# High and low split weights word by word in one buffer, and split products that run from the last column to the first

## The chip, the cores and the metric

The kernel runs on one core of one Trainium2 chip. A run's time is the device time of that core in microseconds. Two runs of the kernel before are shown; the trace is of a third, profiled execution.

## The reference

The reference computes three transformer layers, one after the other, on one sequence of 512 tokens with 1024 channels, all in float32. What matters here is that nearly all arithmetic is products of the activations with weight matrices:

```python
h = rms_norm(x, pre_mix_norm)
proj = h @ w_in                              # 1024 -> 6,688 channels
mix = jnp.concatenate([o_a, o_s], axis=-1) @ w_out      # after gated delta net and SSD
x = x + rms_norm(mix, post_mix_norm)
u = causal_dwconv(h @ w_up, ffn_conv_w, ffn_conv_b)     # 1024 -> 2 * 2816
gate, up = jnp.split(u, 2, axis=-1)
f = (jax.nn.silu(gate) * up) @ w_down                   # 2816 -> 1024
return x + rms_norm(f, post_ffn_norm)
```

The second and third layers have the same form with a stick-breaking attention plus pooling, and a gated linear attention, in place of the first mixer, and each has its own feed-forward part.

## The kernel before

**Tiling.** Activations lie with the channels on the 128 partitions and the 512 tokens along the free axis, so a tensor of 1024 channels is 8 tiles of 128x512 (`tile(t, k)`, 2048 bytes a partition each). Weights come in units: 128 output channels, with 8 tiles (KD, 1024 words a partition) or 11 tiles (HALF, 1408 words, for the down projections) of 128x128.

**Split products.** To keep float32 accuracy with TensorE's faster float32r operands, a value is held as two float32r parts, high and low. A product of a weight tile with an activation tile is three matmuls of 512 columns, one behind the other: high weights by high activations, high by low, low by high. All three add into one PSUM bank. In `multiply` they are lines L255, L256 and L257; `fan` (L231 to L233), `begin_pe` (L1466 to L1468) and `mix_pe` (L2634 to L2636) have the same three. Activations in two parts are HH/HL, MH/ML, PH/PL, DH/DL and FH/FL, whose tiles are read with their 512 columns in rising order.

**How a unit is made.** SyncE loads it into one of four `raw` buffers. ScalarE's `split_hi` (L187) copies it into `whi` as float32r. VectorE's `split_lo` (L193) takes `raw - whi` into `wlo`. There are two `whi` and two `wlo` buffers (SPLIT = 2), each one contiguous run of words, so `split_hi` of unit u waits until TensorE has finished unit u-2 (`unit_done`), `split_lo` waits for `split_hi`, and TensorE waits for `split_lo` (`w_lo_ready`). Ten units at the starts of stages go into `first` buffers and two into `early` buffers, likewise in pairs.

**What else the engines do.** In the up projections VectorE scales a finished bank by the norm factor (L390), makes the low part of the unit after next (L193), and does two convolution taps (L464, L468); ScalarE does the high part (L187), the first tap (L438), and for each pair of units a SiLU (L443) and a copy (L447). In the gated delta net (the "GDN" stretch, up to about 350 us) VectorE also inverts small triangular blocks (L1675, L1678, and a transposing copy L1681).

**Plain products.** Products of plain float32 operands leave two records each in the trace, each with a weight load of its own: L2138 with 512 columns, L1728 with 128 columns, among others.

The order on every engine is the order of the program's text; no scheduler moves anything.

Of the kernel before, what the change touches and what calls it, by code (L numbers as in the profile page):

```python
# [64 lines left out]
def program(nc, x_in, w8, w11, par_in, cst_in, small_in, out, plan):  # L65
    cols = columns()
    ctx = ExitStack()
    with ctx:
# [30 lines left out]
        neg_lower, neg_ones, hidden = (cst[:, k * P:(k + 1) * P] for k in range(12, 15))  # L99
        level = [cst[:, (5 + k) * P:(6 + k) * P] for k in range(7)]  # L100
# [25 lines left out]
        for at0 in (0, 8, 16):  # L126
            first_weights[at0] = [tuple(place(f"first_{n}{at0}_{j}", KD * P, FREE + (at0 + 4 * j + 2 * m) * TILE, F32R)
                                        for m, n in enumerate(("hi", "lo"))) for j in range(2)]
# [27 lines left out]
        NORM_COLUMNS, ALL_PARAMS = 9, 16 * 9  # L156
# [24 lines left out]
        def split_hi(act, u, i, per, kt, first=None, behind=SPLIT):  # L181

            hi = whi[u % SPLIT] if first is None else first[0]
            act.wait_ge(raw_in[u % RAW], at(16 * (u // RAW + 1), i, 16 * per // RAW))
            if u >= behind and first is None:
                act.wait_ge(unit_done, at(u - behind + 1, i, per))
            nc.scalar.activation(hi[:, 0:kt * P], raw[u % RAW][:, 0:kt * P], ACT.Copy).then_inc(w_hi_ready, 1)  # L187

        def split_lo(dve, u, i, per, kt, first=None, behind=SPLIT):

            hi, lo = (whi[u % SPLIT], wlo[u % SPLIT]) if first is None else first
            dve.wait_ge(w_hi_ready, at(u + 1, i, per))
            nc.vector.tensor_tensor(lo[:, 0:kt * P], raw[u % RAW][:, 0:kt * P],  # L193
                                    hi[:, 0:kt * P].bitcast(F32), ALU.subtract).then_inc(w_lo_ready, 1)
# [27 lines left out]
        def fan(pe, c, hi, lo, ready, after=None):  # L222

            u0, n = c["u"], c["fan"]
            w = [c["first"][j] if j < 2 else (whi[(u0 + j) % SPLIT], wlo[(u0 + j) % SPLIT]) for j in range(n)]
            pe.wait_ge(w_lo_ready, u0 + n)
            for k in range(KD):
                pe.wait_ge(ready[0], ready[1] + k + 1)
                for j in range(n):
                    a, (wh, wl) = c["spare"][j], (x[:, k * P:(k + 1) * P] for x in w[j])  # L230
                    nc.tensor.matmul(a[:, :], wh, tile(hi, k), start=k == 0, stop=False)  # L231
                    nc.tensor.matmul(a[:, :], wh, tile(lo, k), start=False, stop=False)  # L232
                    last = nc.tensor.matmul(a[:, :], wl, tile(hi, k), start=False, stop=k == KD - 1)  # L233
                    if k == KD - 1:
                        last.then_inc(unit_done, 1)
                if after and k in after:
                    after[k]()

        def multiply(pe, u, t, i, per, per_t, kt, hi, lo, start=True, stop=True, ready=None, part=None, c=None):
# [11 lines left out]
            for k in range(kt) if part is None else range(kt * part // 4, kt * (part + 1) // 4):  # L251
                if ready:
                    pe.wait_ge(ready[0], ready[1] + k + 1)
                wh, wl = whi[w][:, k * P:(k + 1) * P], wlo[w][:, k * P:(k + 1) * P]
                nc.tensor.matmul(a[:, :], wh, tile(hi, k), start=start and k == 0, stop=False)  # L255
                nc.tensor.matmul(a[:, :], wh, tile(lo, k), start=False, stop=False)  # L256
                last = nc.tensor.matmul(a[:, :], wl, tile(hi, k), start=False, stop=stop and k == kt - 1)  # L257
# [11 lines left out]
        def norm_pe(pe, c):  # L269
# [6 lines left out]
        early = [tuple(place(f"early_{n}{j}", KD * P, FREE + (24 + 4 * j + 2 * m) * TILE, F32R)  # L276
                       for m, n in enumerate(("hi", "lo"))) for j in range(2)]
# [886 lines left out]
        def sb_pool(pool, c):  # L1164
# [15 lines left out]
            nc.gpsimd.tensor_copy(sb_cr[:, P:4 * P], cst[:, 12 * P:15 * P]).then_inc(b_const, 1)  # L1180
# [16 lines left out]
        def sb_pe(pe, c):  # L1197
# [114 lines left out]
            busy(bank[0], whi[(u0 + 11) % SPLIT], 12)  # L1312
# [137 lines left out]
        def begin_pe(pe, c):  # L1450

            for k in range(KD):
# [8 lines left out]
                for m in range(2):  # L1462
# [3 lines left out]
                    nc.tensor.matmul(a[:, :], wh, tile(HH, k), start=k == 0, stop=False)  # L1466
                    nc.tensor.matmul(a[:, :], wh, tile(HL, k), start=False, stop=False)
                    last = nc.tensor.matmul(a[:, :], wl, tile(HH, k), start=False, stop=k == KD - 1)  # L1468
# [672 lines left out]
        def load_l1(sp, c):  # L2141
# [39 lines left out]
            for n, k in enumerate(place_of, 1):  # L2181
# [441 lines left out]
        def mix_pe(pe, c):  # L2623
            for m, (k, h) in enumerate(MIX):
# [5 lines left out]
                for j in range(KD):  # L2630
                    if m in (0, 4):
                        pe.wait_ge(h_ready, c["h"] - 2 * KD + h * KD + j + 1)
                    wh, wl = whi[w][:, j * P:(j + 1) * P], wlo[w][:, j * P:(j + 1) * P]
                    nc.tensor.matmul(a[:, :], wh, tile(hi, j), start=h == 0 and j == 0, stop=False)  # L2634
                    nc.tensor.matmul(a[:, :], wh, tile(lo, j), start=False, stop=False)  # L2635
                    last = nc.tensor.matmul(a[:, :], wl, tile(hi, j), start=False, stop=h == 1 and j == KD - 1)  # L2636
# [342 lines left out]
```

## Time and profile before

| | us |
|---|---|
| median of two runs | 2149.45 (2145.89 to 2153.01) |
| the profiled execution, its own time | 2152.09 |
| its span, first to last instruction | 2150.3 |
| TensorE busy | 2102.0 (98%) |
| VectorE busy | 1212.8 (56%) |
| ScalarE busy | 905.8 (42%) |

The profiled execution is 1.8 us longer than its span and lies inside the range of the two runs. TensorE's busy time is a union of overlapping records, so it shows that the engine had work, not how fast that work went: the distance between the starts of neighbouring matmuls tells that. PEclk, or the granted clock, is the share of 2.4 GHz that TensorE was granted; its mean over the span is 0.993.

### The profile page before, as it was taken

The page shows a single profiled execution, that of the slowest core. Times are in us where ns is not written, and L with a number is a line of the kernel's source. Part 1 is how long each engine was busy: PE and PEld are TensorE (multiplying, and loading weights), DVE is VectorE, ACT ScalarE, POOL GpSimd, SP SyncE. Part 2 cuts the span into 40 slices and gives each one's busy share as a digit, 9 for nine tenths or more (in the row PEclk, how much of TensorE's full clock was granted, in tenths as well). Part 3 has the DMA queues.
Part 4 walks back from the last instruction along what each step waited for, and adds up shares of the span by engine and source line. Part 5 has one row for each costly group of instructions (what it writes and reads, how often), then busy time and mean ns, then how long its engine had stood idle before and what let it go on. Part 6 is the DMA issues. An engine that isn't in the chain of part 4 may idle for free.

```text
span 2150.3 us, 26841 instructions
## 1 busy us (share of the span) xinstructions
PE 2102.0 (98%) x9776; PEld 1702.9 (79%) x9776; DVE 1212.8 (56%) x1663; ACT 905.8 (42%) x1282; POOL 325.0 (15%) x266
## 2 busy tenths in 40 slices
PE   6999999999999999999999999999999999999999
PEld 5778888878868888887766888888878878888887
DVE  5898755755366666225544566653354465666522
ACT  6883444434254444224555444442242254444421
POOL 0001121210112222001302122220000012222200
PEclk9999999999999999999999999999999999999999
DMA  7323222122223333222211333232222122333321
GB/s 235 93 77 93 75 75 79 49 69 69 91 66 98 98 98 115 99 80 69 66 43 40 98 98 96 93 119 95 86 69 89 60 70 97 98 97 96 116 95 66
DMA packets 81481, 188.96 MB, mean 88 GB/s; under 512 B 19824, under 2 KB 40432, under 8 KB 81392
## 3 DMA queue, kind: packets, MB, share of 16 engines
q1 hardware_dynamic: 81392, 187.75, 27.7%
q8 instruction: 59, 0.97, 0.2%
q14 instruction: 30, 0.25, 0.0%
HBM read 178.28 MB, written 9.44 MB: 87 GB/s over the span
## 4 chain that ended last, share of the span: by engine, by line
PE 91%; DVE 5%; ACT 2%; issue 1%; DMA 0%; POOL 0%; SPq 0%; DVEq 0%; ACTq 0%
PE acc L255 23%; PE acc L257 23%; PE acc L256 23%; PE bank L1247 1%; PE bank L231 1%; PE bank L233 1%; PE bank L232 1%; PE acc L2636 1%; PE acc L2634 1%; PE acc L2635 1%; PE bank L2019 1%; PE bank L1728 1%; DVE wlo L193 1%; PE bank L255 1%; PE bank L256 1%
## 5 line engine op out<-in xcount | busy, mean ns | idle before, releaser
L255 PE MATMUL acc<-HH,whi 128*128 128x512 f32 x1600 | 643.6, 402 | 6.9 <-DVE wlo L193 4.3
L257 PE MATMUL acc<-HH,wlo 128*128 128x512 f32 x1600 | 625.7, 391 | 0.0
L256 PE MATMUL acc<-HL,whi 128*128 128x512 f32 x1600 | 624.7, 390 | 0.0
L187 ACT ACTIVATE whi<-raw 128x1024 fp32r<-128x1024 f32 (+1 forms) x293 | 324.0, 1107 | 566.1 <-PE acc L257 536.8
L193 DVE TENSOR_TENSOR wlo<-raw,whi 128x1024 fp32r<-128x1024 f32 (+1 forms) x293 | 400.8, 1369 | 283.0 <-ACT whi L187 283.0
L255 PEld LDWEIGHTS acc<-HH,whi 128*128 128x128 f32 x1600 | 301.9, 189 | 73.8 <-DVE wlo L193 10.3
L257 PEld LDWEIGHTS acc<-HH,wlo 128*128 128x128 f32 x1600 | 301.2, 188 | 64.2
L256 PEld LDWEIGHTS acc<-HL,whi 128*128 128x128 f32 x1600 | 302.0, 189 | 62.6 <-issue 4.1
L255 PE MATMUL acc<-FH,whi 128*128 128x512 f32 x528 | 205.8, 390 | 0.0
L256 PE MATMUL acc<-FL,whi 128*128 128x512 f32 x528 | 205.4, 389 | 0.0
L257 PE MATMUL acc<-FH,wlo 128*128 128x512 f32 x528 | 205.4, 389 | 0.0
L390 DVE TENSOR_TENSOR acc<-acc,rs 128x512 f32<-128x512 f32 x150 | 104.8, 698 | 175.7 <-PE acc L257 175.7
L482 POOL TENSOR_TENSOR taps<-taps,taps 128x512 f32<-128x512 f32 x66 | 85.3, 1292 | 507.5 <-DVE taps L468 452.5
L447 ACT ACTIVATE FH<-taps 128x512 f32 (+1 forms) x66 | 41.8, 633 | 199.3 <-POOL taps L482 199.3
L255 PEld LDWEIGHTS acc<-FH,whi 128*128 128x128 f32 x528 | 99.1, 188 | 20.9 <-issue 0.2
L256 PEld LDWEIGHTS acc<-FL,whi 128*128 128x128 f32 x528 | 99.1, 188 | 20.8 <-issue 0.2
L257 PEld LDWEIGHTS acc<-FH,wlo 128*128 128x128 f32 x528 | 99.1, 188 | 20.5
L345 POOL TENSOR_TENSOR hn<-hn,sq 128x512 f32<-128x512 f32 x24 | 36.7, 1528 | 410.9 <-ACT sq L338 410.9
L468 DVE SCALAR_TENSOR_TENSOR taps<-acc,par,taps 128x510 f32<-128x510 f32 x117 | 87.6, 749 | 14.7 <-DVE taps L464 0.5
L487 POOL TENSOR_TENSOR FL<-taps,FH 128x512 f32 (+1 forms) x66 | 85.5, 1295 | 59.9 <-ACT FH L447 59.9
L438 ACT ACTIVATE taps<-acc,par 128x512 f32<-128x512 f32 x117 | 89.0, 761 | 0.6 <-DVE acc L390 0.6
L464 DVE SCALAR_TENSOR_TENSOR taps<-acc,par,taps 128x511 f32<-128x511 f32 x117 | 86.6, 740 | 0.0
(394 smaller groups left out, 2674.4 us busy)
## 6 DMA issues: line engine op xcount, KB each, us to landing
raw<-w SPq DMA_DIRECT2D x257, 512.0 KB, 3.5
raw<-w SPq DMA_DIRECT2D x48, 704.0 KB, 4.0
X<-x SPq DMA_DIRECT2D x4, 512.0 KB, 5.2
x_dram<-small SPq DMA_DIRECT2D x8, 256.0 KB, 4.7
xt_dram<-small SPq DMA_DIRECT2D x8, 256.0 KB, 4.5
a_dram<-l_am SPq DMA_DIRECT2D x8, 256.0 KB, 3.6
l_xt<-xt_dram SPq DMA_DIRECT2D x8, 256.0 KB, 3.3
l_x<-x_dram SPq DMA_DIRECT2D x8, 256.0 KB, 3.1
```

The lines of the kernel that those rows point to most:

```text
L187: nc.scalar.activation(hi[:, 0:kt * P], raw[u % RAW][:, 0:kt * P], ACT.Copy).then_inc(w_hi_ready, 1)
L193: nc.vector.tensor_tensor(lo[:, 0:kt * P], raw[u % RAW][:, 0:kt * P], hi[:, 0:kt * P].bitcast(F32), ALU.subtract).then_inc(w_lo_ready, 1)
L255: nc.tensor.matmul(a[:, :], wh, tile(hi, k), start=start and k == 0, stop=False)
L256: nc.tensor.matmul(a[:, :], wh, tile(lo, k), start=False, stop=False)
L257: last = nc.tensor.matmul(a[:, :], wl, tile(hi, k), start=False, stop=stop and k == kt - 1)
L390: nc.vector.tensor_tensor(a[:, :], a[:, :], rs[:, :], ALU.mult).then_inc(scaled, 1)
L438: nc.scalar.activation(taps[j][:, :], a[:, :], ACT.Identity, scale=w(2), bias=w(3)).then_inc(tap_ready, 1)
L447: nc.scalar.activation(o, taps[j - 1][:, :], ACT.Copy).then_inc(fh_ready, 1)
L464: nc.vector.scalar_tensor_tensor(out=taps[j][:, 1:S], in0=a[:, 0:S - 1], scalar=w(1), in1=taps[j][:, 1:S], op0=ALU.mult, op1=ALU.add).then ...
L468: nc.vector.scalar_tensor_tensor(out=taps[j][:, 2:S], in0=a[:, 0:S - 2], scalar=w(0), in1=taps[j][:, 2:S], op0=ALU.mult, op1=ALU.add).then ...
L482: nc.gpsimd.tensor_tensor(taps[2 * b][:, :], taps[2 * b][:, :], taps[2 * b + 1][:, :], ALU.mult).then_inc(prod_ready, 1)
L487: nc.gpsimd.tensor_tensor(o, taps[2 * b][:, :], h.bitcast(F32), ALU.subtract).then_inc(f_ready, 1)
```

## The change

It has three parts.

1. The pairs `whi[j]`, `wlo[j]` become one buffer `split[j]`: word 0 is the high part of weight 0, word 1 its low part, word 2 the high part of weight 1, and so on. `parts` gives the two views, each with every second word. So ScalarE writes, VectorE reads and writes, and TensorE loads weights with a step of two words. The `first` and `early` buffers are laid out in the same way.
2. `flipped` reverses the 512 columns of both the activation tile and the PSUM bank in every split product, so column 511 goes first. The result is the same.
3. Where a unit begins in `split[j]` depends on the buffer and the unit's length (`SHIFT`, in words: 64 and 32 for units of 8 tiles, 96 and 16 for 11). The room for it comes from constants that are no longer kept: `cst` is 10 tiles in place of 15, loaded by two transfers in place of one. The start of the free region stays a multiple of 512 bytes from that of HH, and is now a multiple of 2048.

```diff
-        whi = [fixed(f"whi{j}", [P, HALF * P], F32R) for j in range(SPLIT)]
-        wlo = [fixed(f"wlo{j}", [P, HALF * P], F32R) for j in range(SPLIT)]
-        cst = fixed("cst", [P, 15 * P])
+        split = [fixed(f"split{j}", [P, 2 * HALF * P + P], F32R) for j in range(SPLIT)]
+        SHIFT = {KD: (64, 32), HALF: (96, 16)}
+
+        def weights(w, kt):
+
+            o = SHIFT[kt][w]
+            return parts(split[w][:, o:o + 2 * kt * P])
+
+        def parts(pair):
+
+            both = pair.rearrange("p (c m) -> p m c", m=2)
+            return both[:, 0, :], both[:, 1, :]
+
+        def flipped(t):
+
+            return t[:, ::-1]
+
+        cst = fixed("cst", [P, 10 * P])
...
-            hi = whi[u % SPLIT] if first is None else first[0]
+            hi = (weights(u % SPLIT, kt) if first is None else first)[0]
...
-            hi, lo = (whi[u % SPLIT], wlo[u % SPLIT]) if first is None else first
+            hi, lo = weights(u % SPLIT, kt) if first is None else first
...
-                wh, wl = whi[w][:, k * P:(k + 1) * P], wlo[w][:, k * P:(k + 1) * P]
-                nc.tensor.matmul(a[:, :], wh, tile(hi, k), start=start and k == 0, stop=False)
-                nc.tensor.matmul(a[:, :], wh, tile(lo, k), start=False, stop=False)
-                last = nc.tensor.matmul(a[:, :], wl, tile(hi, k), start=False, stop=stop and k == kt - 1)
+                wh, wl = (x[:, k * P:(k + 1) * P] for x in weights(w, kt))
+                nc.tensor.matmul(flipped(a), wh, flipped(tile(hi, k)), start=start and k == 0, stop=False)
+                nc.tensor.matmul(flipped(a), wh, flipped(tile(lo, k)), start=False, stop=False)
+                last = nc.tensor.matmul(flipped(a), wl, flipped(tile(hi, k)), start=False, stop=stop and k == kt - 1)
...
-                    sp.dma_start(cst[:, 2 * P:], cst_in[:, 2 * P:]).then_inc(params_in, 16)
+                    sp.dma_start(cst[:, 2 * P:5 * P], cst_in[:, 2 * P:5 * P]).then_inc(params_in, 16)
+                    sp.dma_start(cst[:, 5 * P:], cst_in[:, 10 * P:]).then_inc(params_in, 16)
```

No instruction changes its place on an engine. On TensorE, in a projection of the second layer, these five rows stood before:

```order
3013 L255 MATMUL acc<-HH,whi_58 128x512
3014 L256 MATMUL acc<-HL,whi_58 128x512
3015 L257 MATMUL acc<-HH,wlo_60 128x512
3016 L255 MATMUL acc<-HH,whi_58 128x512
3017 L256 MATMUL acc<-HL,whi_58 128x512
```

and now, with the high and the low part under one name:

```order
3013 L270 MATMUL acc<-HH,split_58 128x512
3014 L271 MATMUL acc<-HL,split_58 128x512
3015 L272 MATMUL acc<-HH,split_58 128x512
3016 L270 MATMUL acc<-HH,split_58 128x512
3017 L271 MATMUL acc<-HL,split_58 128x512
```

The same instructions stand in the same order; only operands differ. The one instruction more in the whole program is on SyncE, the second transfer of constants near the start.

## Rows read from the trace of the kernel before

**Rows 1.** The page: busy time, granted clock by slice, chain by engine.

```profile
PE 2102.0 (98%) x9776; PEld 1702.9 (79%) x9776; DVE 1212.8 (56%) x1663; ACT 905.8 (42%) x1282; POOL 325.0 (15%) x266
...
PEclk9999999999999999999999999999999999999999
...
PE 91%; DVE 5%; ACT 2%; issue 1%; DMA 0%; POOL 0%; SPq 0%; DVEq 0%; ACTq 0%
```

**Rows 2.** Timeline, first up projection: start us, us, engine, line, operation.

```profile
699.63 0.39 PE L255 MATMUL acc<-HH,whi 128*128 128x512 f32 x1
...
700.08 0.39 PE L257 MATMUL acc<-HH,wlo 128*128 128x512 f32 x1
700.08 0.19 PEld L255 LDWEIGHTS acc<-HH,whi 128*128 128x128 f32 x1
700.31 0.39 PE L255 MATMUL acc<-HH,whi 128*128 128x512 f32 x1
...
705.75 0.39 PE L255 MATMUL acc<-HH,whi 128*128 128x512 f32 x1
```

**Rows 3.** Groups by line and form: the high (L187) and low (L193) parts.

```profile
L193 DVE TENSOR_TENSOR wlo<-raw,whi 128x1024 fp32r<-128x1024 f32 x245 | 322.8, 1319 | 154.8 <-ACT whi L187 154.8
L187 ACT ACTIVATE whi<-raw 128x1024 fp32r<-128x1024 f32 x245 | 257.8, 1054 | 371.7 <-PE acc L257 342.5 <-PE acc L2636 11.9 <-PE bank L233 8.6
L193 DVE TENSOR_TENSOR wlo<-raw,whi 128x1408 fp32r<-128x1408 f32 x48 | 78.0, 1625 | 128.2 <-ACT whi L187 128.2
L187 ACT ACTIVATE whi<-raw 128x1408 fp32r<-128x1408 f32 x48 | 66.2, 1379 | 194.4 <-PE acc L257 194.4
...
L193 DVE TENSOR_TENSOR first_lo<-raw,first_hi 128x1024 fp32r<-128x1024 f32 x10 | 11.8, 1222 | 13.1 <-ACT first_hi L187 13.1
...
L193 DVE TENSOR_TENSOR early_lo<-raw,early_hi 128x1024 fp32r<-128x1024 f32 x2 | 2.4, 1222 | 0.3 <-ACT early_hi L187 0.3
```

**Rows 4.** The chain in order of time, plain float32 products: start us, us, what.

```profile
193.44 0.89 PE bank L1728 x8
...
201.13 0.86 PE bank L2138 x2
```

**Rows 5.** Timeline of VectorE over two units of the up projection.

```profile
701.87 0.70 DVE L390 TENSOR_TENSOR acc<-acc,rs 128x512 f32<-128x512 f32 x1 [0.65 <-PE acc L257]
703.04 1.22 DVE L193 TENSOR_TENSOR wlo<-raw,whi 128x1024 fp32r<-128x1024 f32 x1 [0.48 <-ACT whi L187]
...
705.07 0.75 DVE L468 SCALAR_TENSOR_TENSOR taps<-acc,par,taps 128x510 f32<-128x510 f32 x1
707.31 0.70 DVE L390 TENSOR_TENSOR acc<-acc,rs 128x512 f32<-128x512 f32 x1 [1.49 <-PE acc L257]
708.97 1.55 DVE L193 TENSOR_TENSOR wlo<-raw,whi 128x1024 fp32r<-128x1024 f32 x1 [0.96 <-ACT whi L187]
...
712.75 0.70 DVE L390 TENSOR_TENSOR acc<-acc,rs 128x512 f32<-128x512 f32 x1 [0.67 <-PE acc L257]
```

**Rows 6.** Windows of the GDN and the second up projection: busy us of each engine.

```profile
core 0: us, PE busy (x) PEld busy (x) DVE busy (x) ACT busy (x) POOL busy (x), PEclk, DMA share, GB/s
100.00:172.00 72.00, 68.31 (x342) 54.50 (x341) 69.00 (x139) 52.03 (x81) 3.60 (x4) 1.00 0.32 90
1195.00:1436.00 241.00, 241.00 (x1061) 198.85 (x1060) 151.38 (x175) 100.48 (x133) 54.41 (x42) 1.00 0.31 98
```

**Rows 7.** The same GDN window, instructions of line L193 alone.

```profile
100.00:172.00 72.00, 10.30 (x9) 1.00 0.32 90
```

**Rows 8.** Line L1681: duration ns min/median/max, first and last start, forms.

```profile
L1681 DVE COPY l_blk<-small x3: 1062/1108/1118, 156.4 to 284.5; 48x1024 f32<-48x1024 f32 x2, 32x1024 f32<-32x1024 f32 x1
```

More of the change, by code:

```diff
@@ L97, in program @@
         ident, ones, upper, lower, halves = (cst[:, k * P:(k + 1) * P] for k in range(5))
-        neg_lower, neg_ones, hidden = (cst[:, k * P:(k + 1) * P] for k in range(12, 15))
-        level = [cst[:, (5 + k) * P:(6 + k) * P] for k in range(7)]
+        neg_lower, neg_ones, hidden = (cst[:, k * P:(k + 1) * P] for k in range(7, 10))
+        level = {5 + k: cst[:, (5 + k) * P:(6 + k) * P] for k in range(2)}
         def col(name, k=0, n=1):
@@ L126, in program @@
         for at0 in (0, 8, 16):
-            first_weights[at0] = [tuple(place(f"first_{n}{at0}_{j}", KD * P, FREE + (at0 + 4 * j + 2 * m) * TILE, F32R)
-                                        for m, n in enumerate(("hi", "lo"))) for j in range(2)]
+            first_weights[at0] = [parts(place(f"first_{at0}_{j}", 2 * KD * P, FREE + (at0 + 4 * j) * TILE, F32R)[:, :])
+                                  for j in range(2)]
         acc = [ctx.enter_context(nc.psum_tensor(f"acc{j}", [P, S], F32)) for j in range(2)]
@@ L224, in fan @@
             u0, n = c["u"], c["fan"]
-            w = [c["first"][j] if j < 2 else (whi[(u0 + j) % SPLIT], wlo[(u0 + j) % SPLIT]) for j in range(n)]
+            w = [c["first"][j] if j < 2 else weights((u0 + j) % SPLIT, KD) for j in range(n)]
             pe.wait_ge(w_lo_ready, u0 + n)
@@ L230, in fan @@
                     a, (wh, wl) = c["spare"][j], (x[:, k * P:(k + 1) * P] for x in w[j])
[L231 to L233 removed]
+                    nc.tensor.matmul(flipped(a), wh, flipped(tile(hi, k)), start=k == 0, stop=False)
+                    nc.tensor.matmul(flipped(a), wh, flipped(tile(lo, k)), start=False, stop=False)
+                    last = nc.tensor.matmul(flipped(a), wl, flipped(tile(hi, k)), start=False, stop=k == KD - 1)
                     if k == KD - 1:
@@ L275, in program @@
         NARROW = 32
-        early = [tuple(place(f"early_{n}{j}", KD * P, FREE + (24 + 4 * j + 2 * m) * TILE, F32R)
-                       for m, n in enumerate(("hi", "lo"))) for j in range(2)]
+        early = [parts(place(f"early_{j}", 2 * KD * P, FREE + (24 + 4 * j) * TILE, F32R)[:, :]) for j in range(2)]
         tab_w = place("tab_w", KD * NARROW, FREE + 17 * TILE)
@@ L1311, in sb_pe @@
             pe.wait_ge(w_lo_ready, u0 + 12)
-            busy(bank[0], whi[(u0 + 11) % SPLIT], 12)
+            busy(bank[0], weights((u0 + 11) % SPLIT, KD)[0], 12)
             for i in range(NP):
@@ L1465, in begin_pe @@
                         pe.wait_ge(w_lo_ready, m + 1)
-                    nc.tensor.matmul(a[:, :], wh, tile(HH, k), start=k == 0, stop=False)
-                    nc.tensor.matmul(a[:, :], wh, tile(HL, k), start=False, stop=False)
-                    last = nc.tensor.matmul(a[:, :], wl, tile(HH, k), start=False, stop=k == KD - 1)
+                    nc.tensor.matmul(flipped(a), wh, flipped(tile(HH, k)), start=k == 0, stop=False)
+                    nc.tensor.matmul(flipped(a), wh, flipped(tile(HL, k)), start=False, stop=False)
+                    last = nc.tensor.matmul(flipped(a), wl, flipped(tile(HH, k)), start=False, stop=k == KD - 1)
                     if k == KD - 1:
@@ L2632, in mix_pe @@
                         pe.wait_ge(h_ready, c["h"] - 2 * KD + h * KD + j + 1)
[L2633 to L2636, printed above, removed]
+                    wh, wl = (x[:, j * P:(j + 1) * P] for x in weights(w, KD))
+                    nc.tensor.matmul(flipped(a), wh, flipped(tile(hi, j)), start=h == 0 and j == 0, stop=False)
+                    nc.tensor.matmul(flipped(a), wh, flipped(tile(lo, j)), start=False, stop=False)
+                    last = nc.tensor.matmul(flipped(a), wl, flipped(tile(hi, j)), start=False, stop=h == 1 and j == KD - 1)
                 last.then_inc(unit_done, 1)
```

6 lines of the change are left out of this document (3 added, 3 removed).

## The prediction

> **What bounds the kernel now.** I read the page first. TensorE is busy 98% of the span and makes 91% of the chain that ends last, VectorE 5% and ScalarE 2% [rows 1]. The granted clock stands at 9 tenths or more in every slice, so the engine runs at its upper level of 2.4 GHz almost throughout, and no clock effect is to be won or lost. With TensorE bound and never idle (241.00 us busy of 241.00 in the second up projection [rows 6]), the only question that matters is how long one matmul of 512 columns takes from its start to the next one's start. The record of a matmul is 0.39 us long, but it overlaps its neighbours. The timeline gives the distance: from the L255 at 699.63 to the one at 705.75 lie nine rounds of three matmuls, so 6.12 us / 27 = 226.7 ns each [rows 2]. At 2.4 GHz 512 columns take 512 / 2.4 = 213.3 ns, so each split matmul has 13.4 ns over.
>
> How many there are follows from the low parts made: 245 + 10 + 2 units of 8 tiles and 48 of 11 [rows 3]. That is 257 x 8 + 48 x 11 = 2584 tiles, by three, 7752 matmuls. By 226.7 ns they are 1757 us of the 2150.3 us span. The 13.4 ns over are worth 104 us in all, which is the most that any change of the operands' layout could give.
>
> Is that surplus a price of every weight load? The plain float32 products say no. Two records of L2138, 512 columns each, take 0.86 us on the chain, so 0.43 us a record [rows 4]. That is twice 215 ns, as if each record ran its 512 columns twice, with one load of 128x128 weights for each record. Each such run has under 2 ns over, though a weight load lies beside it as well. What differs in a split matmul is that 512 float32 words are fetched in 213 ns, not in 430, while 128 words of weights are fetched by the load that starts in the same moment (L255's load at 700.08, with the matmul L257 at 700.08) [rows 2]. So I read the 13.4 ns as the two fetches getting in each other's way: 13.4 ns is 32 columns' time at 2.4 GHz, and the load fetches 128 words, so as if one in four of its words took a column's slot. Nothing in the rows proves that; it is the reading that fits both kinds of product.
>
> **Part 1 and 2: interleaving and flipping, on TensorE.** A load that takes every second word moves through memory twice as fast as before. A weight load of 128 words cannot take longer than the distance of the plain 128-column products, 0.89 us / 8 = 111 ns [rows 4], so its step of one word was at least 128 x 4 bytes / 111 ns = 4.6 bytes a ns. With a step of two words it is 9.2 or more, and the activations' fetch is 512 x 4 / 213.3 = 9.6 bytes a ns. The two fetches now go at about the same pace. Bounds from the rows: each matmul takes between 213.3 ns, the columns alone, and 226.7 ns, if nothing is changed; a loss is not excluded, see the rivals. I take 215 ns, half of the L2138 record, since that is what this engine reaches when a load does not disturb it. The saving is 11.7 ns x 7752 = 90.7 us, of which I count TensorE's share of the chain: 0.91 x 90.7 = 82.5 us. The rest falls where another engine is late, above all between 100 and 172 us, where VectorE is busy 69.00 of 72 us and TensorE isn't full [rows 6].
>
> The Trainium skill speaks against this saving. "TensorE: Matmul & The Clock Gate", section "Part 2: What happens when you issue a matmul", has two independent read ports, so that loading the next weights takes nothing from a running matmul; "SBUF — State Buffer", section "Who interferes with whom", says that TensorE never waits for anyone. By that rule the surplus is no clash and stays, which is the first rival. The same page's Part 1 gives warm back-to-back matmuls of 512 columns 215.7 ns, which the 226.7 ns of this trace don't reach.
>
> **Part 1 on ScalarE and VectorE.** ScalarE's copy takes 1054 ns for 1024 words [rows 3] and VectorE's subtraction 1222 ns where GpSimd leaves it alone, 1319 ns in the mean. ScalarE now writes, and VectorE reads and writes, every second word. No row has this step. The nearest is L1681, a copy that reads one word in 32 of a run and takes 1108 ns for 1024 words [rows 8]: about the rate of L193, so a step in a read costs nothing there, and the lower bound is 0 (a gain is excluded, since the same words are moved). The upper bound is that the step makes a word cost twice. The words cost (1379 - 1054) / 384 = 0.85 ns on ScalarE, and on VectorE (1222 - 698) / 512 = 1.02 ns by L390's 0.70 us for 512 [rows 3, 5], so 0.87 and 1.05 us more for a unit. I take nothing for ScalarE and 0.6 us for VectorE, nearer to the middle than to L1681, because L1681 steps only in its read.
>
> Who hides it? In the up projection two units take 712.75 - 701.87 = 10.88 us, in which VectorE waits 1.49 + 0.67 us for TensorE [rows 5], 2.16 us in all. The 48 faster matmuls take 0.56 us of that away and leave 1.60, or 0.8 us a unit: just enough for the 0.6. What is late next is the end of L468, which frees the bank. In the down projections a unit has 33 matmuls (7.5 us) and little else. In the GDN window VectorE sets the pace, with nine low parts [rows 7]: 9 x 0.6 = 5.4 us, bounds 0 and 9 us. I put all of it on the path.
>
> The Trainium skill has two answers here. "Vector Engine (DVE) Microarchitecture Reference", section "5.2 Measured stream behaviour on trn2", wants runs of two adjacent words and gives 1.71 ns a column where the output hops at each element, which as an estimate is 0.7 us more for 1024 words; "SBUF — State Buffer", section "Door 1", asks for two hits on a line of 16 bytes, which a step of two float32 words still has, so nothing. The sum would be 1 us higher by the one and 5 us lower by the other.
>
> **Part 3.** The second transfer of constants on SyncE stands behind the first weight units, and together the two move less than the one did. Nothing waits for it that does not wait now; I count nothing. Nothing else is moved, and no wait is added.
>
> **Sum.** 2152.1 (the profiled execution's own time) - 82.5 + 5.4 = 2075, and 2076 with rounding; the median of the shown runs is 2.6 us lower than that execution, which is inside the two runs' distance, so I don't correct for it. A measurement of this kernel can tell about 2% (43 us) from no change.
>
> **The rivals.**
>
> *The surplus is not a clash.* It is a fixed price of a split matmul with its weight swap. For it: it is the same 226.7 ns whatever buffer or stage I look at. Against it: the plain products' 2 ns. Then only VectorE's cost is left: 2152 to 2161, I say 2156.
>
> *The load gets slower with its step.* If a word in two costs the load twice its time, 2 x 111 = 222 ns [rows 4], the load becomes longer than the 213.3 ns of columns and sets the distance. 226.7 - 222 = 4.7 ns, x 7752 x 0.91 = 33 us, so 2119 + 5 = 2124. Against it: the plain load's 111 ns are an upper bound.
>
> *Slower: the strided writes make VectorE the bound.* Place: up projections, 132 units. The high part must be done before the low part, so both costs add in a unit. At the upper bounds two units get 2 x (0.87 + 1.05) = 3.84 us against 1.60 us of slack, so a pair takes 10.88 - 0.56 + 2.24 = 12.56 us: 1.68 more, x 66 = 111 us. GDN adds 9. The other 7752 - 3168 = 4584 matmuls still gain 11.7 ns x 0.91 = 49 us. Total 2152 + 111 + 9 - 49 = 2223. It begins to cost from 0.8 us a unit on and cancels the whole gain from about 1.4 us on. For it: nothing in the trace has this step in a write. Against it: L1681.
>
> *Slower, too:* if a reversed column order halves the rate of the fetch or of the write into PSUM, a matmul takes the 0.43 us of an L2138 record and the time rises far above 3000 us. I give it little.
>
> **How the numbers follow.** Forecast, 2055 to 2100: 0.5. The slow load or a surplus that goes only in part, 2100 to 2145: 0.13. The fixed surplus, 2145 to 2165: 0.18. Slower cases: 0.19. The range runs from 2048, where the whole 13.4 ns go (104 x 0.91 = 95 us) and hardly anything is added, to 2165, and leaves out the slower cases. Faster by over 2% is under 2106: the forecast and a third of the partial case, 0.54. Within 2%: 0.27. Slower by over 2%: 0.19.
>
> **What would show it.** The distance of neighbouring split matmuls in the up projection: 215 ns right, 227 the first rival, 222 with the load's start spaced alike the second. The mean of the high and low parts against 1054 and 1319 ns. VectorE's wait for TensorE in the up projection: near 1 us for two units if right, gone in the slower case, with TensorE idle behind L193 or L468. I would be wrong above all if the fetches do not clash, or if they clash more when they go side by side.

## The result, and the profile after

The changed kernel takes 2202.25 us (median of two runs, 2200.14 to 2204.36), against 2149.45 before: 1.0246 times, interval 1.0161 to 1.033. In a second set of runs, in alternation with the kernel before, it was 2205.91 against 2151.8 us, 1.0242 times, interval 1.0225 to 1.0259. It is slower, where I had forecast 2076 us. The time moves with the granted clock, whose mean over a run lies between 0.992 and 0.998: runs of equal clock in the second set are 57 to 59 us apart (2210.06 against 2151.3 to 2152.86 at 0.993, 2207.9 against 2150.48 at 0.994).

The page of the changed kernel, busy time, granted clock and chain, answers to [rows 1]:

```profile
PE 2156.9 (98%) x9776; PEld 1758.1 (80%) x9776; DVE 1211.7 (55%) x1663; ACT 939.1 (43%) x1282; POOL 320.3 (15%) x266
...
PEclk9999999999999999999999999999999999999999
...
PE 91%; DVE 5%; ACT 2%; issue 1%; DMA 0%; POOL 0%; SPq 0%; DVEq 0%; ACTq 0%
```

The shape is the same: the same engine bounds it, at nearly the same clock (0.996 in the mean, where it was 0.993), with the same share of the chain. TensorE's busy time grew by 54.9 us, and the span by 52.3 us. So TensorE does not sit idle longer; its own work takes longer, first because the split matmuls stand further apart. The timeline of the changed kernel, first up projection, has nine rounds of three between these two starts, as [rows 2] had:

```profile
699.82 0.40 PE L270 MATMUL acc<-HH,split 128*128 128x512 f32 x1
...
706.12 0.40 PE L270 MATMUL acc<-HH,split 128*128 128x512 f32 x1
```

6.30 us / 27 = 233.3 ns, where it was 226.7. In columns at 2.4 GHz (0.4167 ns) that is 560 in place of 544, for a tile of 512.

The groups of the changed kernel for the high (L202) and the low part (L208), answering to [rows 3]:

```profile
L208 DVE TENSOR_TENSOR split<-raw,split 128x1024 fp32r<-128x1024 f32 x245 | 314.6, 1286 | 179.2 <-ACT split L202 179.1
...
L202 ACT ACTIVATE split<-raw 128x1024 fp32r<-128x1024 f32 x245 | 285.9, 1169 | 391.1 <-PE acc L272 355.2 <-PE bank L248 14.7 <-PE acc L2651 12.0
```

ScalarE's copy takes 1169 ns in place of 1054; VectorE's subtraction is no slower (1286 against 1319). Over two units of the up projection VectorE still waits for TensorE, as in [rows 5]:

```profile
709.12 0.70 DVE L404 TENSOR_TENSOR acc<-acc,rs 128x512 f32<-128x512 f32 x1 [0.87 <-PE acc L272]
...
714.72 0.70 DVE L404 TENSOR_TENSOR acc<-acc,rs 128x512 f32<-128x512 f32 x1 [1.52 <-PE acc L272]
```

2.39 us in 11.20, where it was 2.16 in 10.88. And where VectorE had set the pace, the GDN window, it is as busy as in [rows 6], with TensorE's longer matmuls filling idle time:

```profile
100.00:172.00 72.00, 68.99 (x340) 56.25 (x339) 69.03 (x138) 53.42 (x82) 3.59 (x4) 1.00 0.32 90
```

The stages tell the same. Starts of the first row of each, in us of the timeline, before and after:

| stage | before | after | longer by |
|---|---|---|---|
| start of the SSD's output products (DH) | 506.4 | 506.3 | 0 |
| first down projection | 854.0 | 865.7 | 11.8 |
| first product after it | 981.1 | 999.7 | 6.9 |
| second down projection | 1436.6 | 1468.9 | 13.7 |
| first product after it | 1556.3 | 1592.1 | 3.5 |
| third down projection | 2027.3 | 2076.1 | 13.0 |
| end | 2150.3 | 2202.6 | 3.5 |

The first row says less than it seems, because these two traces had unlike clocks there: between 172 and 350 us the granted clock was 0.96 in the trace before and 0.98 in the one after (the third number from the end of each row; the third row is of `changed_again`, the trace of the second set).

```profile
172.00:350.00 178.00, 169.96 (x1019) 147.72 (x1018) 115.39 (x252) 75.84 (x119) 31.46 (x21) 0.96 0.26 74
```

```profile
172.00:350.00 178.00, 170.07 (x1026) 149.24 (x1026) 116.43 (x254) 77.54 (x120) 31.14 (x21) 0.98 0.26 74
```

```profile
172.00:350.00 178.00, 170.57 (x1010) 150.06 (x1009) 116.02 (x252) 75.91 (x117) 32.45 (x22) 0.95 0.25 73
```

`changed_again` has the mean clock of the trace before, 0.993, and there the start of the output products lies at 511.9 us, 5.5 us later than before. That stretch holds 52 multiplied units, 1248 split matmuls; by 6.6 ns they are 8.2 us.

The second and third down projections grew by 3.5 us each, which is their 528 split matmuls by 6.6 ns. The first grew by 6.9 us, and the other 3.4 us are not in split matmuls but stand in front of the first product after it. In two places, this one and the start of the first up projection, `first_units` gives TensorE 18 filler products, and a third place, in the second layer's mixer, has 12. Nobody reads their results. They take their 512 columns from a weight buffer:

```python
        def busy(out, w, n):
            for _ in range(n):
                nc.tensor.matmul(out[:, :], w[:, 0:P], w[:, 0:S], start=True, stop=True)
```

In the changed kernel `w` is a view with every second word, so the 512 columns have that step too. After the first down projection, before and after:

```profile
975.98 4.68 PE L220 MATMUL bank<-first_hi 128*128 128x512 f32 x18
```

```profile
991.19 8.72 PE L235 MATMUL bank<-first 128*128 128x512 f32 x18
```

Their distance went from about 227 to 453 ns. From the last split matmul before them to the first one behind them it is 10.17 us in place of 6.80, in both places with 18, and at the third place it is 11.38 in place of 9.05: 9.1 us in all. In the kernel with the columns reversed and separate buffers (`flip_only`, below) all three stay as before (6.81, 6.80 and 9.00 us).

### The profile page after: what moved, and what is told of

Its sections match the earlier page's. It is cut to its first block, busy times and chain, and to the rows that moved or that the text cites. A ratio compares the mean times of both kernels' runs of the same rounds, so it can differ in the third digit from the quotient of the medians.

```text
span 2202.6 us, 26842 instructions
## 1 busy us (share of the span) xinstructions
PE 2156.9 (98%) x9776; PEld 1758.1 (80%) x9776; DVE 1211.7 (55%) x1663; ACT 939.1 (43%) x1282; POOL 320.3 (15%) x266
## 4 chain that ended last, share of the span: by engine, by line
PE 91%; DVE 5%; ACT 2%; issue 1%; DMA 0%; POOL 0%; SPq 0%; DVEq 0%; ACTq 0%
PE acc L270 23%; PE acc L271 23%; PE acc L272 23%; PE bank L1261 1%; PE bank L247 1%; PE bank L248 1%; PE acc L2651 1%; PE bank L246 1%; PE acc L2649 1%; PE acc L2650 1%; PE bank L235 1%; PE bank L2033 1%; PE bank L1742 1%; DVE split L208 1%; PE bank L270 1%
## 5 line engine op out<-in xcount | busy, mean ns | idle before, releaser
L270 PE MATMUL acc<-HH,split 128*128 128x512 f32 x1600 | 655.7, 410 | 6.2 <-DVE split L208 3.9
L271 PE MATMUL acc<-HL,split 128*128 128x512 f32 x1600 | 637.0, 398 | 0.0
L272 PE MATMUL acc<-HH,split 128*128 128x512 f32 x1600 | 636.9, 398 | 0.0
L202 ACT ACTIVATE split<-raw 128x1024 fp32r<-128x1024 f32 (+1 forms) x293 | 359.3, 1228 | 588.3 <-PE acc L272 552.4
L208 DVE TENSOR_TENSOR split<-raw,split 128x1024 fp32r<-128x1024 f32 (+1 forms) x293 | 392.7, 1341 | 315.5 <-ACT split L202 315.5
L270 PEld LDWEIGHTS acc<-HH,split 128*128 128x128 f32 x1600 | 313.6, 196 | 71.9 <-DVE split L208 10.0
L272 PEld LDWEIGHTS acc<-HH,split 128*128 128x128 f32 x1600 | 313.3, 196 | 62.5
L271 PEld LDWEIGHTS acc<-HL,split 128*128 128x128 f32 x1600 | 313.7, 196 | 60.5 <-issue 4.0
L270 PE MATMUL acc<-FH,split 128*128 128x512 f32 x528 | 209.7, 397 | 0.0
L272 PE MATMUL acc<-FH,split 128*128 128x512 f32 x528 | 209.3, 396 | 0.0
L271 PE MATMUL acc<-FL,split 128*128 128x512 f32 x528 | 209.3, 396 | 0.0
L271 PEld LDWEIGHTS acc<-FL,split 128*128 128x128 f32 x528 | 102.3, 194 | 21.2 <-issue 0.2
L270 PEld LDWEIGHTS acc<-FH,split 128*128 128x128 f32 x528 | 102.3, 194 | 21.1 <-issue 0.2
L272 PEld LDWEIGHTS acc<-FH,split 128*128 128x128 f32 x528 | 102.3, 194 | 20.9
```

The source lines that it names most:

```text
L270: nc.tensor.matmul(flipped(a), wh, flipped(tile(hi, k)), start=start and k == 0, stop=False)
L271: nc.tensor.matmul(flipped(a), wh, flipped(tile(lo, k)), start=False, stop=False)
L272: last = nc.tensor.matmul(flipped(a), wl, flipped(tile(hi, k)), start=False, stop=stop and k == kt - 1)
```

## The experiments

Kernels sent together shared one chip and the runs of the kernel before on it (median 2150.1, 2150.2, 2150.2, 2151.8, 2143.45 and 2149.84 us in the six sets). The distances are worked out as above, 27 matmuls apart unless said.

**The columns reversed, and nothing else** (separate buffers):

```diff
-                nc.tensor.matmul(a[:, :], wh, tile(hi, k), start=start and k == 0, stop=False)
+                nc.tensor.matmul(flipped(a), wh, flipped(tile(hi, k)), start=start and k == 0, stop=False)
```

(and so all split products)

> The kernel before with the column order of every split product reversed and nothing else (separate high and low buffers, constants as before). Theory A, the direction in which the activations are fetched against the weight load is what costs: the distance of two split matmuls in the up projections goes from 226.7 to 233 ns or beyond and the kernel to about 2200 us. Theory B, the weight load's step of two words is what costs: it stays at 226.7 ns and 2150 us. Theory C, only both together cost: 226.7 ns here as well.

2190.7 us, 1.0193 times (1.0176 to 1.021). Its timeline in the first up projection:

```profile
700.26 0.40 PE L259 MATMUL acc<-HH,whi 128*128 128x512 f32 x1
...
706.56 0.40 PE L259 MATMUL acc<-HH,whi 128*128 128x512 f32 x1
```

6.30 us, so 233.3 ns: reversing alone brings the whole change of distance. B and C fall as the only cause.

**The shared buffers alone** (with their starts and the shorter constants):

```diff
-            return t[:, ::-1]
+            return t[:, :]
```

> The changed kernel with the columns in rising order again; the shared buffers, their start offsets and the shorter constants stay. Theory A (direction): 226.7 ns and about 2150 us, with ScalarE's copy still at 1169 ns. Theory B (the load's step): 233 ns and about 2200 us. Theory C (only both together): 226.7 ns, as by A; it is told from A by the run with the columns reversed alone.

2196.75 us, 1.0219 times (1.0199 to 1.0239). That is no part of A's expectation: the shared buffers cost as much by themselves. Its timeline in the first up projection, and its group of ScalarE's copy:

```profile
699.92 0.39 PE L270 MATMUL acc<-HH,split 128*128 128x512 f32 x1
...
706.18 0.40 PE L270 MATMUL acc<-HH,split 128*128 128x512 f32 x1
```

```profile
L202 ACT ACTIVATE split<-raw 128x1024 fp32r<-128x1024 f32 x245 | 277.1, 1133 | 392.3 <-PE acc L272 356.1 <-PE bank L248 14.8 <-PE acc L2651 12.3
```

6.26 us / 27 = 231.9 ns, and the copy takes 1133 ns. By stage the mean is 233.0 ns in the up and 231 in the down projections. Each half costs about 2%, and both together 2.4%: the two costs don't add. The shared buffers' 46.7 us hold the 9.1 us of the slower fillers, so their split matmuls cost less than the reversal does.

**Every unit at word 0 of its buffer:**

```diff
-        SHIFT = {KD: (64, 32), HALF: (96, 16)}
+        SHIFT = {KD: (0, 0), HALF: (0, 0)}
```

> The changed kernel with every unit starting at word 0 of its shared buffer. If the starts steer which words clash, the distances in the up projections (buffers 0 and 1 apart) move from 233 to 235 ns by several ns up or down, and differ between the two buffers. If the starts don't matter, 233 to 235 ns and 2200 us stay.

2220.91 us, one run. First down projection:

```profile
899.82 0.40 PE L270 MATMUL acc<-FH,split 128*128 128x512 f32 x1
...
906.22 0.40 PE L270 MATMUL acc<-FH,split 128*128 128x512 f32 x1
```

6.40 us / 27 = 237.0 ns (236.7 in the mean of the stage), the same in both buffers. Start 0 puts the weights at 0 and 128 words modulo 256 against the activations' tiles, for buffer 0 and 1, so at a multiple of 512 bytes in both. So the starts matter a little: in most stages such an alignment is worse than the chosen ones.

**Operands of one column.** Only in the feed-forward parts:

```diff
+        def mv(t):
+            return t[:, 0:1].to_broadcast([P, S]) if "m" in mode[0] else t
+        def wt(t):
+            return t[:, 0:1].to_broadcast([P, P]) if "w" in mode[0] else t
```

> The kernel before, but with operands of one column read again and again: in the first up and down projections the activations (one word for all 512 columns), in the second the weights (one column for all 128), in the third both. These products are then not the reference's. If the 13.4 ns over are a clash of the two fetches in memory, taking one fetch's walk away changes the distance, towards 213 to 216 ns (or far up, if the one word lies in the other's way all the time). If they are a fixed price of a split matmul, all three stages keep 226.7 ns.

First down projection (activations of one column), then the second (weights of one column) and the third (both):

```profile
900.24 0.38 PE L263 MATMUL acc<-FH,whi 128*128 128x512 f32 x1
...
906.07 0.38 PE L263 MATMUL acc<-FH,whi 128*128 128x512 f32 x1
...
1479.88 0.40 PE L263 MATMUL acc<-FH,whi 128*128 128x512 f32 x1
...
1486.13 0.39 PE L263 MATMUL acc<-FH,whi 128*128 128x512 f32 x1
...
2050.23 0.38 PE L263 MATMUL acc<-FH,whi 128*128 128x512 f32 x1
...
2056.06 0.38 PE L263 MATMUL acc<-FH,whi 128*128 128x512 f32 x1
```

5.83 us / 27 = 215.9 ns with the activations' walk taken away; 6.25 / 27 = 231.5 ns with the weights' walk taken away; 5.83 / 27 = 215.9 ns again with both. A fixed price of a split matmul is ruled out, and with it my first rival: the same three matmuls with their three loads run at 216 ns if the activations are one word, and what the weights' addresses do moves the rest. The whole kernel ran 2125.27 us.

**Which side of the reversal, and a step in the activations.** Separate buffers, one variant for each feed-forward part:

```diff
+        def mv(t, k):
+            if "2" in mode[0]:                 # third part: every second word of two tiles
+                ...
+            return tile(t, k)[:, ::-1] if "r" in mode[0] else tile(t, k)    # second part
+        def to(a):
+            return a[:, ::-1] if "w" in mode[0] else a[:, :]                # first part
```

> The kernel before (separate buffers) with one variant for each feed-forward part, whose products are then not the reference's. First part: the bank is written from the last column to the first, the activations are read in rising order. Second part: only the activations are read from the last column to the first. Third part: the activations are read with a step of two words over two tiles (the first tile of each row of tiles as before). If the direction of the fetch against the weight load costs the 6.7 ns, the first part stays at 226.7 ns and the second goes to 233.3; if the reversed write into PSUM costs them, the other way round. Third part: if the pace at which the fetches pass matters, it moves away from 226.7 ns, up if a step costs bandwidth of its own.

First down projection (only the bank is written in reverse), second (only the activations are read in reverse):

```profile
899.99 0.39 PE L268 MATMUL acc<-FH,whi 128*128 128x512 f32 x1
...
906.11 0.39 PE L268 MATMUL acc<-FH,whi 128*128 128x512 f32 x1
...
1500.07 0.40 PE L268 MATMUL acc<-FH,whi 128*128 128x512 f32 x1
...
1506.37 0.40 PE L268 MATMUL acc<-FH,whi 128*128 128x512 f32 x1
```

6.12 us, 226.7 ns, for the reversed write: it is free. 6.30 us, 233.3 ns, for the reversed read: that is the cost. With a step of two words in the activations the distance in the third part became 450 to 459 ns, half the pace (the first tile of each unit, read as before, kept 230 to 255), and the kernel 2480.43 us. The fillers' 453 ns are the same case. In both the bank is written in plain order, so it is the read that costs.

**Other starts, twelve of them.** The changed kernel with starts by stage and buffer, once as it is and once with rising columns:

```diff
+        STAGES = {KD: ((69, (16, 64)), (153, (32, 96)), (246, (96, 240))), HALF: ((113, (16, 32)), (197, (32, 64)), (290, (64, 96)))}
```

> The changed kernel with other starts in the shared buffers in the three up and the three down projections: taken by the word at which the weights begin, modulo 256 words (1024 bytes), against the activations' tiles, the up projections get 16 and 192, 32 and 224, 96 and 240 (buffer 0 and 1), the down projections 16 and 160, 32 and 192, 64 and 224. The changed kernel has 64 and 160, 96 and 144. Theory A, side by side the two fetches keep a distance that the start sets: one of the twelve starts gives distances near 216 ns and another 237 ns or more. Theory B, they drift against each other in any case and the start moves only the remainder: all stay between 230 and 238 ns.

2196.1 us, one run. In the first down projection:

```profile
900.07 0.40 PE L274 MATMUL acc<-FH,split 128*128 128x512 f32 x1
...
906.37 0.40 PE L274 MATMUL acc<-FH,split 128*128 128x512 f32 x1
```

Again 233.3 ns, and so it was in every feed-forward stage and both buffers. Theory B: no start brings the distance down. Nor is the alignment to 512 bytes the only one that is worse. In the changed kernel's second and third up projections the units in buffer 1 (start 32) have 236.5 ns and those in buffer 0 have 233.4, while in the first up projection both have 233.3, with the same buffers and the same tiles.

> The same starts with the columns in rising order, so that the two fetches run against each other. By both theories they pass one another whatever the start is, so all stages stay near the 231 to 233 ns of the run with the shared buffers and rising columns. If the start matters here too, the stages differ by more than 2 ns.

2190.23 us, one run; the units of the feed-forward parts had about 230 to 233.5 ns, a few 235.5, and the two buffers of a stage differed by up to 3 ns. So with rising columns the start takes part, which neither theory had. It does not decide alone: in `interleave_only`, units in the same buffer of an up projection have 233.4 and 235.4 ns by turns.

> The changed kernel with starts of 16 and 64 words for units of 8 tiles and 16 and 32 for units of 11 tiles. If the starts 64 and 32 are what lifts the second and third up projections from 233.3 to 235 ns, those come back to 233.3 ns and the kernel is 4 to 8 us faster than the changed one, about 2196 us. If the sweep's 2196 us were chance, 2202 us.

```diff
-        SHIFT = {KD: (64, 32), HALF: (96, 16)}
+        SHIFT = {KD: (16, 64), HALF: (16, 32)}
```

2202.26 us, 1.0238 times (1.0221 to 1.0256), beside the changed kernel's 1.0242 in the same set. The starts of the change are not what makes it slow. Whether the sweep's 2196 us were chance this run does not tell. It left the second and third up projections at 235.0 ns in the mean, as in the changed kernel (now buffer 0 has the 236.5), while the sweep had 233.3 there, and 1.7 ns x 2112 is 3.6 us of the 6.

> The changed kernel itself, run in alternation with the kernel before on one chip: 2202 us, so that its distance to the two runs beside it has an interval.

Its result stands with the first one, in the section on the result.

**The third part of the change alone:** ten constants, two transfers, the same start of the free region.

> The kernel before with the third part of the change alone: ten constants in place of fifteen, loaded by two transfers, and the start of the free region where the changed kernel has it (a pad of 256 words makes up for the missing room of the shared buffers). Every theory: 2150 us, within 2 us, and 226.7 ns. If it isn't, the alignment of the free region takes part.

2151.56 against 2151.8 us, 0.9992 times (0.9983 to 1.0002). It costs nothing, as predicted.

**The weight load's step without shared buffers.** Steps of 2, 3 and 4 words in the three feed-forward parts:

```diff
+        def wt(t, k):
+            n = mode[0]
+            s = min(k * P, KD * P - n * P)
+            return t[:, s:s + n * P].rearrange("p (c m) -> p m c", m=n)[:, 0, :] if n > 1 else t[:, k * P:(k + 1) * P]
```

> The kernel before, with the weights of the three feed-forward parts read from its contiguous buffers with a step of 2, 3 and 4 words, columns rising; the products are then not the reference's, and no engine writes with a step. If the load's step alone costs (and not what ScalarE and VectorE do to the shared buffers), the first part goes from 226.7 to 231 to 233 ns, as with the shared buffers and rising columns. Steps of 3 and 4: above that if a faster passing clashes more often, back near 227 if only two words a step is special.

2189.13 us, one run. The down projections, step 2, 3, 4:

```profile
900.25 0.39 PE L262 MATMUL acc<-FH,whi 128*128 128x512 f32 x1
...
906.55 0.39 PE L262 MATMUL acc<-FH,whi 128*128 128x512 f32 x1
...
1500.29 0.39 PE L262 MATMUL acc<-FH,whi 128*128 128x512 f32 x1
...
1506.65 0.39 PE L262 MATMUL acc<-FH,whi 128*128 128x512 f32 x1
...
2100.12 0.40 PE L262 MATMUL acc<-FH,whi 128*128 128x512 f32 x1
...
2106.47 0.40 PE L262 MATMUL acc<-FH,whi 128*128 128x512 f32 x1
```

233.3, 235.6 and 235.2 ns. The step of the load costs by itself, whoever wrote the buffer; a larger one costs little more.

**Other orders of the activations.** Activations and bank in the same order of runs, so that the result stays the reference's:

```diff
+        def runs(t):
...
+            n, m = mode[0]
+            return t.rearrange("p (c m n) -> p m c n", m=m, n=n)
```

> The kernel before, with the 512 columns of activations and bank taken in hops, the same in both, so that the products are the reference's: in the first feed-forward part pairs of words and every second pair (step of 16 bytes), in the second four words and every second four (step of 32 bytes), in the third pairs and every eighth pair (step of 64 bytes). If only the direction of the two fetches decides, all parts keep 226.7 ns. If the pace at which they pass decides, the parts differ, and one may lie below 226.7 ns, down to 216. If hops cost the fetch bandwidth, as single words with a step of two did (about 450 ns), they go up towards 430.

> The kernel before with columns of activations and bank taken in longer runs: four words and every fourth four (64-byte hops) in the first feed-forward part, eight words and every second eight in the second, sixteen words and every second sixteen in the third; the products are the reference's. Runs of four words with 32-byte hops gave 233.3 ns. If an order of lines exists that meets the weight load less often than the plain rising one, one part lies under 226.7 ns; if rising lines are the best order, all lie at 226.7 or above.

> As the runs of four words before (separate buffers, products as the reference's), with larger hops: every eighth four (128 bytes) in the first feed-forward part, every sixteenth (256 bytes) in the second, every thirty-second (512 bytes) in the third. 64-byte hops gave 223.3 ns in the up projection, 32-byte hops 233.3. If the clash falls with the speed at which the two fetches pass, these lie under 223.3 ns; if it depends on which lines the hops reach, they scatter on both sides of 226.7.

Runs of four words with hops of 64 bytes, first up projection of the second of these kernels:

```profile
699.61 0.39 PE L264 MATMUL acc<-HH,whi 128*128 128x512 f32 x1
...
705.65 0.38 PE L264 MATMUL acc<-HH,whi 128*128 128x512 f32 x1
```

6.04 us / 27 = 223.7 ns, under the kernel before. All nine, in up projections, from such rows:

| run of words | hop in bytes | distance, ns |
|---|---|---|
| plain rising (before) | | 226.7 |
| 2 | 16 | 451 |
| 2 | 64 | 431 |
| 4 | 32 | 233.3 |
| 4 | 64 | 223.7 |
| 4 | 128 | 246.7 |
| 4 | 256 | 278 |
| 4 | 512 | 268 |
| 8 | 64 | 232.2 |
| 16 | 128 | 240.4 |

The distances neither rise nor fall with the hop, so a speed of passing alone does not explain them; one of the nine lies below the plain order. The bank was written in the same order as the activations were read, so these rows do not tell a cost of the read from one of the write. That holds for the pairs above all: only for single words (above) was the read alone changed. The three kernels took 2838.14, 2181.09 and 2328.51 us, one run each. In the down projection the same 64-byte hops gave 226.7 ns in the mean, no gain.

**The best order in the whole kernel**, for units of 8 tiles, with separate buffers and rising columns in the down projections:

```diff
+        def fours(t):
+            return t.rearrange("p (c m n) -> p m c n", m=4, n=4)
...
+            order = fours if kt == KD else (lambda t: t)
-                nc.tensor.matmul(a[:, :], wh, tile(hi, k), start=start and k == 0, stop=False)
+                nc.tensor.matmul(order(a[:, :]), wh, order(tile(hi, k)), start=start and k == 0, stop=False)
```

> The kernel before (separate buffers, rising columns in the down projections), with activations and bank of all products of 8-tile units taken four words at a time, every fourth four (64-byte hops), four passes over the tile; the products are the reference's. In one feed-forward part this gave 223.3 in place of 226.7 ns. 3.4 ns by 257 x 24 = 6168 matmuls is 21 us; with the share of 0.78 of a changed distance that the reversed columns brought to the end, 16 us less than the kernel before, about 2135 us. If the 223.3 ns held only for that stage's addresses, no difference.

```profile
699.90 0.39 PE L260 MATMUL acc<-HH,whi 128*128 128x512 f32 x1
...
705.93 0.39 PE L260 MATMUL acc<-HH,whi 128*128 128x512 f32 x1
```

223.3 ns here, and 2136.17 us against 2149.84: 0.9936 times (0.9923 to 0.995). It beats both kernels, but not by the distances of the expectation. In the second up projection the distance is that of the kernel before:

```profile
1299.96 0.39 PE L260 MATMUL acc<-HH,whi 128*128 128x512 f32 x1
...
1306.08 0.39 PE L260 MATMUL acc<-HH,whi 128*128 128x512 f32 x1
```

6.12 us / 27 = 226.7 ns, and the third has 226.6 in the mean. In the first, the last four units went back to about 226.6 as well. The buffers, the tiles and the order are the same in all of these units, so what decides between 223.3 and 226.7 is not the addresses alone. From the start of the SSD's output products to the end the trace is only 6.5 us shorter than before (2136.5 - 499.1 against 2150.3 - 506.4). Part of the 13.7 us between the medians is clock: runs of equal granted clock are about 10 us apart (2141.2 against 2151.02 to 2152.02 at 0.993, 2138.26 against 2148.51 at 0.995).

## Why the prediction was wrong, point by point

*What bounds the kernel, and which number decides:* right. Both kernels are set by the distance of split matmuls, and most of the difference is a change of it. Behind the start of the SSD's output products the changed kernel is 52.4 us longer (1696.3 us against 1643.9); 9.1 of these are the fillers, for which my sum had no term.

*The surplus is a clash of two fetches:* right as far as it goes. With the activations held at one word the distance fell to 215.9 ns, 0.9 above the 215 that I had read from the L2138 records [rows 4], and a step in the weights alone moved it to 233.3, so what either fetch reads changes it. The Trainium skill's rule in "SBUF — State Buffer", section "Who interferes with whom", that TensorE never waits, does not hold for TensorE against itself: 10.8 of the 226.7 ns depend on what its own two fetches read.

*That equal pace in the same direction ends the clash:* this is the step that failed. I wrote that fetches going side by side keep their distance and that a clash isn't repeated. It carried the whole saving of 90.7 us. The runs show a loss in its place. The reversed read alone takes the distance from 226.7 to 233.3 ns, the load's step of two alone takes it to 231.9 in the shared buffers and 233.3 in separate ones, and both together leave it at 233.3 or a little above. No run shows which way the load walks through its words. That doesn't save the step: at a step of two, the equal pace that I reckoned with, one of the two column orders must be the one in its direction, and the rising one has 230 to 235 ns, the reversed one 233 to 237. Of the twelve starts of the sweep not one came below 233.3. My bounds, 213.3 to 226.7 ns, took the kernel before as the worst case, and "a loss is not excluded" led to no rival with a price of this size (I named a clash made worse as the way to be wrong, and gave it no term); a surplus raised by half, from 13.4 to 20.0 ns, wasn't in my list, so the range ended at 2165. Its lower end was off as well: 2152 less the 95 us is 2057, and 2048 takes the 104 without the factor 0.91.

*What of the distance reaches the end:* I took TensorE's share of the chain, 0.91. For the reversed columns 6.6 ns x 7752 = 51 us became 40.6 us between the medians, 0.79. Part of this gap is the clock again: at 0.994 that kernel's run took 2193.39 us and those of the kernel before 2149.94 to 2150.77, 43 us, 0.84. By stage, from the start of the SSD's output products on, its trace is 39.4 us longer (1683.3 against 1643.9), and 7752 - 1248 = 6504 split matmuls by 6.6 ns are 42.9 us: 0.92, close to what I had taken. The rest is absorbed in the first 506 us, where other work is late; the changed kernel at equal clock loses 5.5 of 8.2 us there, and a pause of TensorE's split matmuls at 474 us shrank from 10.81 to 9.17.

*ScalarE and VectorE:* I took nothing for ScalarE and 0.6 us for VectorE's low part. It is 0.115 us on ScalarE and nothing on VectorE (1223 ns in place of 1222 for the units in `first` buffers). The slower case through VectorE, the third rival, did not happen: VectorE waits for TensorE more than before. So the kernel is slower for another reason than the slower rival gave. No row shows that ScalarE's longer copy reached the end.

*What I did not look at:* the fillers. I wrote that nothing else is moved, but `busy` reads the weight buffers, and its 48 products got the step of two in their 512 columns, at 453 in place of 227 ns each. The changed kernel lies 11.6 us beyond the reversal alone (2202.3 - 2190.7), and its trace 13.0 us from the SSD's output products on (52.4 - 39.4). The fillers are 9.1 of these, and the second and third up projections, with about 235.0 ns in the mean, 1.7 more than the reversal's 233.3, are 1.7 ns x 2112 = 3.6.

*The third part and the order of instructions:* right, nothing (0.9992 times).

What stays open is the rule behind the clash. The runs give distances for directions, steps, hops and starts, and I have no model that gives all of them: held at one column, the weights still cost 231.5 ns, though with the activations at one column too it is 215.9. And the same buffers, tiles and order gave 223.3 and 226.7 ns, or 233.3 and 236.5, in different stages, so something beside the addresses takes part that no run names.

## What to carry to other kernels

Where TensorE is full, compare the distance of neighbouring starts with the columns' own time, and treat what is over as something that the order and place of both operands can change: hold one operand at one column for a stage to see how much of it is to be had. When a change reshapes two streams that disturb each other, the state before is not the worst case; bound it on both sides and try one stage for each variant in a single kernel, since a model of the clash gave me the wrong sign. Measure the distance in every stage before you multiply it by a count: the best order here held its 223.3 ns in one up projection of three. Look up every reader of a buffer that you lay out anew, fillers too. And compare runs of equal granted clock where a difference is under 1%.

## What was not expected of the hardware

- The weight load and the activations' fetch of one engine disturb each other: 226.7 ns plain, 215.9 with the activations at one word, 231.5 with the weights at one column, 233.3 with reversed columns, 236.7 with reversed columns and the shared buffers at start 0. At one set of addresses two values can occur (223.3 and 226.7, 233.3 and 236.5).
- A step of two words in float32r activations halves the pace: 450 to 459 ns, and 453 in the fillers. With activations and bank in the same order, pairs of words had 431 and 451 ns and fours 223.7 to 278; how much of the pairs' is the bank's was not tried.
- Writing a bank in reverse costs nothing by itself (226.7 ns).
- Writing every second word costs ScalarE 1133 in place of 1054 ns for 1024 words, and 1169 when TensorE reads in reverse as well, though reversing alone left its copy at 1053. VectorE reads and writes such words at its usual pace (1286 against 1319 ns).
